# First stage of a two-block transformer kernel: the turn of the modulation row between high and low products, and the row's copy ahead of the weight split

## The reference

```python
c_act = jax.nn.silu(c)
for l in range(DEPTH):
    mod = c_act @ w_ada[l] + b_ada[l]
    sh1, sc1, g1, sh2, sc2, g2 = jnp.split(mod[:, None, :], 6, axis=-1)
    h = rms_norm(x, mix_norm_pre[l]) * (1.0 + sc1) + sh1
    a_q, a_f, a_i, a_g, b_q, b_k, b_v, c_a, c_g = split_cols(h @ w_in[l], IN_SPLITS)
    ...
    yc = conv_module(c_a, c_g, conv_w[l], conv_b[l], conv_ln_g[l], conv_ln_b[l])
```

## Time and profile before

| what | value |
| --- | --- |
| median of three runs | 3157.11 us |
| lowest and highest | 3154.61 and 3159.85 us |
| time of the profiled execution | 3164.62 us |
| its span, first to last instruction | 3162.8 us |
| TensorE busy | 3091.1 us, 98% of the span |
| VectorE busy | 2370.3 us, 75% |
| ScalarE busy | 1334.4 us, 42% |
| mean granted TensorE clock | 0.995 of full speed |

### The profile page before, as it was taken

One profiled execution on the slowest core, in us unless ns is written; L12 is line 12 of the kernel. 1 busy time (PEld: TensorE's weight loads), 2 busy tenths in 40 slices (PEclk: granted clock), 3 DMA queues, 4 the chain that ended last, 5 costly groups with the idle time before them and its releaser, 6 DMA issues.

```text
span 3162.8 us, 55850 instructions
## 1 busy us (share of the span) xinstructions
PE 3091.1 (98%) x24202; PEld 2930.6 (93%) x24202; DVE 2370.3 (75%) x2843; ACT 1334.4 (42%) x1459; POOL 1.8 (0%) x10
## 2 busy tenths in 40 slices
PE   7999999999999999999999999999999999999997
PEld 6899999999999989998988999989889999999997
DVE  4799876688887779999978766644667667777766
ACT  3343344434444443343464334521365444444444
POOL 0000000000000000000000000000000000000000
PEclk9999999999999999999999999999999999999999
DMA  9874444488894887777754774354333575665743
GB/s 391 336 215 168 165 156 150 171 335 348 326 360 160 292 307 261 282 255 291 295 209 181 286 275 154 121 217 156 138 133 132 181 268 193 219 234 201 259 178 136
DMA packets 106418, 722.64 MB, mean 228 GB/s; under 512 B 11677, under 2 KB 15389, under 8 KB 27197
## 3 DMA queue, kind: packets, MB, share of 16 engines
q1 hardware_dynamic: 100368, 703.64, 60.3%
q10 hardware_dynamic: 5806, 15.43, 1.6%
HBM read 712.41 MB, written 6.55 MB: 227 GB/s over the span
## 4 chain that ended last, share of the span: by engine, by line
PE 88%; DVE 6%; DMA 3%; ACT 2%; issue 1%; ACTq 0%; DVEq 0%
PE gemm L1063 39%; PE gemm L1072 19%; PE gemm L1106 10%; PE gemm L1111 5%; DMA sb_raw<-stream 2%; DVE sb_parts L1820 2%; PE gemm L1108 1%; PE mix L1063 1%; ACT sb_parts L554 1%; PE mix L1323 1%; PE mix L1610 1%; DMA sb_arena<-x_t 1%; DVE sb_arena L1875 1%; PE gemm L1239 1%; PE mix L1072 1%
## 5 line engine op out<-in xcount | busy, mean ns | idle before, releaser
L554 ACT ACTIVATE sb_parts<-sb_raw 128x2048 fp32r<-128x2048 f32 (+2 forms) x489 | 899.9, 1843 | 1457.5 <-PE gemm L1072 949.0
L1820 DVE TENSOR_TENSOR sb_parts<-sb_raw,sb_parts 128x2048 fp32r<-128x2048 f32 (+2 forms) x489 | 1072.0, 2194 | 301.1 <-PE gemm L1072 146.9
L1063 PE MATMUL gemm<-op_h,sb_parts 128*128 128x256 f32 x7232 | 868.8, 277 | 1.1 <-ACT sb_parts L554 0.6
L1063 PEld LDWEIGHTS gemm<-op_h,sb_parts 128*128 128x128 f32 x7232 | 845.5, 188 | 2.8 <-issue 0.8
L1072 PE MATMUL gemm<-op_h,sb_parts 128*128 128x256 f32 x3616 | 451.0, 277 | 0.0
L1072 PEld LDWEIGHTS gemm<-op_h,sb_parts 128*128 128x128 f32 x3616 | 430.8, 188 | 0.0
L1106 PE MATMUL gemm<-op_up,sb_parts 128*128 128x512 f32 x1536 | 403.4, 392 | 6.0 <-DVE op_up L2449 4.0
L1106 PEld LDWEIGHTS gemm<-op_up,sb_parts 128*128 128x128 f32 x1536 | 260.2, 188 | 49.7 <-DVE op_up L2449 5.7
L1801 DVE CUSTOM_DVE_ANT_0 sb_raw<-sb_raw,sb_arena,sb_vec 128x2048 f32<-128x2048 f32 x96 | 224.4, 2348 | 1.4 <-DMA sb_raw<-stream 0.2
L1111 PE MATMUL gemm<-op_up,sb_parts 128*128 128x256 f32 x1728 | 216.9, 276 | 0.0
L1111 PEld LDWEIGHTS gemm<-op_up,sb_parts 128*128 128x128 f32 x1728 | 210.3, 188 | 5.5
(11 more groups left out here) (366 smaller groups left out, 3505.9 us busy)
## 6 DMA issues: line engine op xcount, KB each, us to landing
sb_raw<-stream SPq DMA_DIRECT2D x597, 1024.0 KB, 4.9
sb_raw<-stream SPq DMA_DIRECT2D x64, 704.0 KB, 4.5
sb_arena<-stream SPq DMA_DIRECT2D x14, 1024.0 KB, 8.8
sb_arena<-stream SPq DMA_DIRECT2D x10, 768.0 KB, 8.5
sb_raw<-stream SPq DMA_DIRECT2D x6, 768.0 KB, 8.1
sb_arena<-c_rows ACTq DMA_DIRECT2D x3, 1024.0 KB, 7.2
bias_rows<-sb_arena ACTq DMA_DIRECT2D x1, 2304.0 KB
sb_arena<-x_t ACTq DMA_DIRECT2D x4, 512.0 KB, 18.9
```

The costliest lines, as they stand in the source:

```text
L554: act.activation(parts[:, b % 2, 0, 0:kt, :], slot_of(slot)[:, 0:kt, :], ACT.Copy).then_inc(hi_ready, 1)
L1063: ins = pe.matmul(out, l, r, start=(opens and i == 0 and x is xh), stop=False, skip_group_check=True)
L1820: dve.tensor_tensor(parts[:, b % 2, 1, 0:kt, :], slot_of(slot)[:, 0:kt, :], parts[:, b % 2, 0, 0:kt, :].bitcast(F32), ALU.subtract).then_i ...
```

## The change

The diff in full:

```diff
@@ block scalar @@
             for r in range(1, KT + 2):
+                if 2 <= r < KT:
+                    copy_row(r)
                 if r >= 2:
                     split_high(r - 2)
-                if 2 <= r < KT:
-                    copy_row(r)
                 if r <= KT:
                     high_tile(opH[:, 0], hf0, mod1, 0, r - 1)
@@ block tensor @@
-            def branch_c_round(k):
+            def branch_c_round(k, between=lambda: None):
                 pe.wait_ge(hi_ready, k + 1)
                 pe.wait_ge(h_part, k + 1)
                 slot, uses = use(G_AT[k])
                 if k < KT - 1:
                     branch_c_part(k, range(6), 0, (0, 1))
+                    between()
                     pe.wait_ge(taken[slot], uses + 1)
                     branch_c_part(k, range(1), 1, (0,)).then_inc(hi_used, 1)
                     branch_c_part(k, range(1, 6), 1, (0,)).then_inc(block_done, 1)
...
-                if r >= 2:
-                    branch_c_round(r - 2)
                 if r == 3:
                     pe.wait_ge(brow_ready, 1)
-                if r < KT:
+                if r >= 2:
+                    branch_c_round(r - 2, (lambda: turn(r)) if r < KT else (lambda: None))
+                elif r < KT:
                     turn(r)
```

## The result

The change makes the kernel slower: 3173.60 us in the median of nine runs (3169.07 to 3182.02), against 3159.34 us for the kernel before in nine runs beside them (3152.8 to 3170.7). The ratio is 1.0041, with a 95% interval of 1.0028 to 1.0054, which is 13 us (9 to 17). The profiled execution after took 3173.60 us with a span of 3171.8 us.

What follows compares the result with a forecast made beforehand. Bound by a chain between engines, loads close behind. Thirteen rounds of 7.56 us instead of 6.70 from 44.4 us give +9.9, less 0.45 in the tail: +9.5 us, 3166.6 us, range 3161.5 to 3171.0.

Steps and rivals of the forecast that it cites:

- The release: From the end of ScalarE's split to the first high product: taken as 0.20 us, with 0.05 and 0.23 for the range.
- the turn between two groups: Turn between high and low products: 1.73 us together with the low products, at worst some 0.1 us more.
- The wait for `brow_ready`: Ahead of round 3's high products: covered, as VectorE is there before the split; uncovered under 1 us, once.
- the tail: After the last round of the first stage: `split_low(15)` no longer late, 0.45 us less.
- the wait for `ada_cols`: VectorE's wait in each round: disappears, but was shorter than what ScalarE now puts in.
- The share of the loads: DMA load share in the first stage: below 1, from 1.01, with loads idle for part of each round.
- The second rival: Much slower: TensorE's clock at half rate in eleven rounds, +60 us, about 3227 us; chance 0.04.
- 12.2 us at little over half busy: Stretch before 29.6 to 42.4 us, matmuls busy 6.70 of 12.20 us, clock 0.99: used against the slow clock.
- The first, not slower: First stage: split stays hidden, taking out the 1.50 us shows, loads decide; 2.6 us sooner, 3154.5 us; chance 0.08.
- point of decision: For the not-slower case, split and its release together must cost under 0.82 us, where they are 1.68.
- gain of 2.6 us: Not-slower case: first stage ends sooner by the G tile's 2.85 us lead less the release of 0.23.
- the load's reserve: The G tile of 122.79, late in the first stage, was 2.85 us early at 6.70 us a round.

Runs made afterwards that it cites:

- more standing: Kernel after the change, with ScalarE's copy of the row done four times in rounds 4 to 15: 3196.65 us in one execution.
- TensorE's half alone: Kernel after, with ScalarE's split put back ahead of its copy: 3158.58 us, ratio 0.9991; run a second time, 3160.77 us, ratio 0.9977.
- split in halves: Kernel after, with splits of weight tiles 0 to 14 in two instructions, TensorE starting three banks on the first: 3164.25 us, ratio 1.0003.

## Why the prediction was right or wrong, point by point

**Right: what the change does to the round.** The chain `ada`, copy, split, high products, turn, low products was forecast at 7.56 us a round. At full clock it is 7.52 or 7.41. Term by term: `ada` to copy 1.15 (57.95 to 59.10), copy to split 0.17, split 1.47, 24 high products 2.82 (60.80 to 63.62), all as forecast. The release was 0.06 us (60.74 to 60.80) where I took 0.20: I chose the row with the same releaser over the row of the same line, and the second was right. Turn and low products took 1.85 us (63.62 to 65.47) instead of 1.73: the turn between two groups costs 0.12, the upper end I had kept for it. The two errors cancel.

**Right: the edges.** Counted from `ada` of round 2, its split moved by less than 0.2 us. The wait for `brow_ready` cost nothing: the view names it once, 1.07 us until 45.91 in round 3, but VectorE had done it at 45.48 and the split of that round ended at 45.81, so it was covered as forecast; and the tail is shorter than before (146.3 to 155.52 against 132.75 to 142.49, 9.2 instead of 9.7 us), where I had 0.45 us. VectorE and the loads are not late.

**Wrong without a price: VectorE's wait.** I had the wait for `ada_cols` disappear. It stayed, 19.5 us in 13 waits, since the turn comes late with the whole row; VectorE is off the path, so nothing hangs on it. The share of the loads was to fall below 1, which it did in the mean (0.96 from 44 to 140 us) though not in each round.

**Wrong: the clock.** This is the step that failed. The second rival had it, but as all eleven rounds or none, at +60 us and a chance of 0.04; the forecast had no term for it. In fact four of the twelve rounds 4 to 15 are long, by 1.5 us each (9.0 against 7.5): 6.0 us. Thirteen rounds at 7.56 us from 44.4 were forecast; they took 103.3 us (43.02 to 146.3), 5.0 us more than 98.3. That is 6.0 us for the clock, less 1.0 for rounds that were 7.48 us in the mean. With the clock's term the sum would have been some 15 us.

Where the argument against it went wrong: I compared shares of busy time, and read from 12.2 us at little over half busy with a clock of 0.99 that three quarters busy were safe. But those 12.2 us were the ones just ahead of the fall. The row should have counted for the rival. I also read from the Trainium skill, "TensorE: Matmul & The Clock Gate", the section "HAM oscillation — how this bites in real kernels", that short stands don't matter. The runs say otherwise: with 1.77 us in a round of 7.5 the clock came down in three or four of the twelve rounds 4 to 15. The next section of that page of the Trainium skill, "A second HAM failure mode: psum-queue depth-cycling", has the clock oscillate, in another kernel, where TensorE idles briefly but often between groups of matmuls. With that the trace agrees in kind (mean clock 0.95 from 44 to 140 us after, 0.86 with more standing), and it was the one to weigh; it gives no price.

**The range.** It ended at 3171.0, and the median was 3173.6. Of the 7.0 us between it and the forecast, 2.2 lie in the reference (the kernel before had 3159.34 in nine runs, 3157.11 in the three I had); the other 4.8 are about the clock's 6.0 us less the 1.0. That split of the medians is a sum and not a measurement: the ratio's interval, 9 to 17 us, still holds the forecast of 9.5. What shows the error is the stage, of which the profiled execution is no guide by its time: it took 3173.60 us, and 3174.1 was forecast for it. That is luck, for its stage ended at 155.52 us and not at 152.0 (142.49 and 9.5), and the later stages took 4 us less than before.

**Rivals.** The first, not slower, needed a split that stays hidden, and it did not. Its round of 5.57 us is what TensorE's half alone shows, 5.67 to 5.75 us in the rounds 4 to 8. Its point of decision was 0.82 us for split and release together, where they are 1.68. With the split in halves 0.98 us of the two are left in the row (106.67 to 107.65); by that working the round is 5.88 and 0.98, 6.86 us, and it was 6.83. Its gain of 2.6 us was too small: with ScalarE's old order the stage is 5 us shorter, since the rounds 4 to 8 run at 5.7 us, which I had not looked at because I took the load's reserve from the end of the stage alone.

**Not settled.** Why the clock falls in just those rounds, and not in others of the same standing, the runs don't say. Each of them changes the length of the stand and TensorE's share of work in the round together, so they don't tell which of the two counts. Nor was the distance between 1.22 and 1.77 us of standing searched.

## What to carry to other kernels

An engine that runs ahead may owe that lead to the order of two short instructions. Before one that waits is moved forward, look at what is queued behind it and whether somebody else's chain begins there; here 1.5 us of a split went from hidden to exposed in each of thirteen rounds, beside a turn moved to free a 1.5 us wait that was no longer on the path then. And a short stand of TensorE, repeated each round, has a second price in its clock: give it a term of its own, in part of the rounds, and not a rival of all or nothing. Where the stand can't be avoided, dummy matmuls in it are worth trying, as they gave back 5.9 us of the stage here.

## What was unexpected of the hardware

Besides the clock, matmuls have two pitches at a granted clock of 1.00. The same 48 matmuls of a weight tile, from the timelines of the kernel before and of TensorE's half alone, both about 885 us into the kernel:

```profile
884.05 2.05 PE L1072 MATMUL gemm<-op_merged,sb_parts 128*128 128x256 f32 x16
885.93 3.93 PE L1063 MATMUL gemm<-op_merged,sb_parts 128*128 128x256 f32 x32
889.70 2.04 PE L1072 MATMUL gemm<-op_merged,sb_parts 128*128 128x256 f32 x16
```

```profile
883.11 1.98 PE L1072 MATMUL gemm<-op_merged,sb_parts 128*128 128x256 f32 x16
884.92 3.79 PE L1063 MATMUL gemm<-op_merged,sb_parts 128*128 128x256 f32 x32
888.55 1.98 PE L1072 MATMUL gemm<-op_merged,sb_parts 128*128 128x256 f32 x16
```

From one group of 16 to the next is 5.65 us in the first and 5.44 us in the second, 0.118 and 0.113 us a matmul. One pitch mostly holds for a hundred us or more and then changes, not at the same places in every execution. By the length of the groups of 16 from 150 us on (1.98 us, or 2.04 and more), 237 of 337 have the short pitch in the profile before, 256 of 337 in the one after, 212 of 337 in the first of TensorE's half and 228 of 335 in the second. The first of TensorE's half had the long one until 865 us, the kernel before only until 618. Each tile is worth 0.21 us, so 19 tiles are 4.0 us and 25 tiles are 5.3, which is as large as the whole gain of TensorE's half. It is also the size of what was left open above: the profile after was only 9.0 us above the profile before, while its stage was 14.6 us longer and began 1.6 us sooner, so the later stages took 4 us less. That the pitch is the reason is a sum of this kind and was not tried. The rounds of 7.41 and 7.52 us differ by the same two pitches in the 24 high products, 2.72 us in round 4 after (53.39 to 56.11) and 2.82 in round 5; in this stage the pitch can change from one round to the next. What switches between them is open.
